# Attention heads in pairs on alternating row halves, and the bias added by VectorE while it takes the minimum

## What is computed

```
# layer 1 (odd): forgetting attention
log_f  = log_sigmoid(x @ w_f + forget_b)               # (S, 8)
cum    = cumsum(log_f, axis=1).transpose(0, 2, 1)
logits = q.k / sqrt(64) + cum[:, :, q0:q1, None] - cum[:, :, None, :q1]
probs  = softmax(where(causal, logits, -1e30));  y = probs @ v
# beside it: GLU -> causal depthwise conv (31 taps, 512 channels) -> LayerNorm -> swish

# layers 2, 3 (hybrid): a softmax over three dilated key patterns,
# equal to one softmax with a fixed bias log(count of patterns) per distance;
# beside it gated linear attention (4 heads), chunkwise
```

## Time and profile before

| | |
|---|---|
| Time, median of 3 runs | 1244.8 us (1244.3 to 1246.14) |
| Span of the profiled execution, first to last instruction | 1240.9 us |
| The profiled execution's own time around it | not given; its span is 3.9 us under the median of the runs |
| TensorE busy | 1216.8 us, 98% |
| VectorE, ScalarE, GpSimd busy | 763.0, 601.5, 37.8 us |
| Attention of layer 1 | about 340.5 to 380 us |
| Attention of layers 2 and 3 | about 682.3 to 705.1 and 1001 to 1024 us |

### The profile page before, as it was taken

How to read it: one execution, slowest core, us unless ns; L and a number is a source line. 1 busy time by engine, 2 the same in 40 slices (tenths; PEclk the granted TensorE clock), 3 DMA queues, 4 the chain that set the end, 5 groups by cost and what they waited for, 6 DMA issues and landing times.

```text
span 1240.9 us, 16942 instructions
## 1 busy us (share of the span) xinstructions
PE 1216.8 (98%) x5874; PEld 995.6 (80%) x5874; DVE 763.0 (61%) x1009; ACT 601.5 (48%) x911; POOL 37.8 (3%) x69
## 2 busy tenths in 40 slices
PE   7999999999999999999999999999999999999997
PEld 5778888888878788888778788888887878888886
DVE  5587545545976855554677766555465776755541
ACT  5455444525663544442465555444356563644430
POOL 0000000000000000000100110000010001000000
PEclk9999999999989999999999999999999999999999
DMA  8567666634701585573465239556626532765540
GB/s 283 169 204 228 219 196 196 222 108 157 247 22 60 180 282 172 179 242 122 136 204 161 70 105 292 173 179 216 213 74 202 181 105 86 232 208 172 178 159 34
DMA packets 162637, 212.99 MB, mean 172 GB/s; under 512 B 15817, under 2 KB 106601, under 8 KB 162576
## 3 DMA queue, kind: packets, MB, share of 16 engines
q1 hardware_dynamic: 155792, 201.44, 51.1%
q10 hardware_dynamic: 6784, 10.75, 2.8%
HBM read 211.09 MB, written 1.05 MB: 171 GB/s over the span
## 4 chain that ended last, share of the span: by engine, by line
PE 87%; DVE 5%; DMA 2%; ACT 2%; POOL 2%; issue 1%; ACTq 1%; SPq 0%; POOLq 0%; DVEq 0%
PE ps L538 25%; PE ps L540 25%; PE ps L539 25%; DMA raw<-ev_w_in 2%; PE ps L938 2%; PE ps L814 2%; DVE w_lo L1363 1%; PE ps L895 1%; PE ps L641 1%; PE ps L872 1%; PE ps L649 1%; PE ps L871 1%; POOL stat L1833 1%; PE ps L879 1%; ACT w_hi L990 1%
## 5 line engine op out<-in xcount | busy, mean ns | idle before, releaser
L1363 DVE TENSOR_TENSOR w_lo<-raw,w_hi 128x1024 fp32r<-128x1024 f32 x380 | 450.3, 1222 | 129.9 <-ACT w_hi L990 127.1
L990 ACT ACTIVATE w_hi<-raw 128x1024 fp32r<-128x1024 f32 x380 | 385.5, 1055 | 137.2 <-PE ps L540 72.7
L538 PE MATMUL ps<-w_hi,a_hi 128*128 128x512 f32 x1040 | 414.2, 398 | 4.2 <-ACT e_pc L1062 2.1
L540 PE MATMUL ps<-w_hi,a_lo 128*128 128x512 f32 x1040 | 406.8, 391 | 0.0
L539 PE MATMUL ps<-w_lo,a_hi 128*128 128x512 f32 x1040 | 405.7, 390 | 0.0
L538 PEld LDWEIGHTS ps<-w_hi,a_hi 128*128 128x128 f32 x1040 | 195.9, 188 | 46.1 <-issue 2.5
L540 PEld LDWEIGHTS ps<-w_hi,a_lo 128*128 128x128 f32 x1040 | 195.6, 188 | 42.2
L539 PEld LDWEIGHTS ps<-w_lo,a_hi 128*128 128x128 f32 x1040 | 196.1, 189 | 38.5
L538 PE MATMUL ps<-w_hi,h_hi 128*128 128x512 f32 x480 | 189.2, 394 | 0.9 <-DVE h_lo L1758 0.8
L540 PE MATMUL ps<-w_hi,h_lo 128*128 128x512 f32 x480 | 187.4, 390 | 0.0
L539 PE MATMUL ps<-w_lo,h_hi 128*128 128x512 f32 x480 | 187.3, 390 | 0.0
(11 more groups left out here) (205 smaller groups left out, 803.5 us busy)
## 6 DMA issues: line engine op xcount, KB each, us to landing
raw<-ffn_w_in SPq DMA_DIRECT2D x176, 256.0 KB, 4.3
raw<-w_in SPq DMA_DIRECT2D x96, 256.0 KB, 3.1
raw<-ffn_w_out SPq DMA_DIRECT2D x88, 256.0 KB, 4.1
raw<-w_gate SPq DMA_DIRECT2D x88, 256.0 KB, 3.6
raw<-w_up SPq DMA_DIRECT2D x88, 256.0 KB, 4.4
raw<-w_down SPq DMA_DIRECT2D x88, 256.0 KB, 4.1
raw<-od_w_in SPq DMA_DIRECT2D x40, 256.0 KB, 2.9
raw<-ev_w_in SPq DMA_DIRECT2D x32, 256.0 KB, 4.9
```

The source lines that it names most:

```text
L538: nc.tensor.matmul(ps[:, bank, :], hi, wh, start=first, stop=False)
L540: return nc.tensor.matmul(ps[:, bank, :], lo, wh, start=False, stop=last)
L990: nc.scalar.activation(w_hi[:, v.slot, :], raw[:, v.raw, :], ACT.Copy).then_inc(w_high, 1)
L1363: V.tensor_tensor(w_lo[:, v.slot, :], raw[:, v.raw, :], w_hi[:, v.slot, :].bitcast(F32), ALU.subtract).then_inc(w_low, 1)
```

## The change

- **Pairs.** `pair_logits(j)` computes near for heads 2j and 2j+1 and then wide for both, on the two row halves in turn. It waits for VectorE's `lows` of the pair before. TensorE's list becomes: `pair_logits(0)`, (linear_values), then for each j: `pair_logits(j+1)`, `head_turn(2j)`, `head_turn(2j+1)`, in layer 1 eight taps, `head_values(2j-2)`, `head_values(2j-1)`.
- **Bias.** The bias matmuls and their constants go. VectorE's `head_lows` reads the scores from PSUM, adds the bias, writes the sum to `probs` (now four buffers, in SBUF) and takes the minimum, in one instruction a part. ScalarE's exponentials work in place on `probs`.
- **Forget sums.** `cum` (8 x 256) is written to DRAM and read back broadcast to all partitions as `o_bias` (128 x 8 x 384, 1.5 MB), on ScalarE's DMA queue. GpSimd adds the causal mask in two instructions. `o_bias` lies over `rows[1]`, `rows[2]` and `nbuf`, so one load of a norm's row moves from layer 1's input projection to behind its attention.
- **Evictions.** In the hybrid layers ScalarE now copies even heads into `probsT`, VectorE odd ones. In layer 1 ScalarE copies all.
- **Feeds and convolution.** In the hybrid layers no unit is fed during attention; four are, after it. In layer 1 ScalarE feeds one unit for each pair, at its end. VectorE's convolution steps before attention go from 33 to 48.

```diff
@@ TensorE
+            def pair_logits(l, j):
+                if j:
+                    pe.wait_ge(lows.sem, lows.at(l, 2 * j - 1))
+                for i in range(2):
+                    r = slice(HD * i, HD * (i + 1))
+                    nc.tensor.matmul(tb[:, i, 0:P], qT[r, j, 0:P], kT[r, j, 0:P], start=True, stop=True)
+                for i in range(2):
+                    r = slice(HD * i, HD * (i + 1))
+                    nc.tensor.matmul(tb[:, i, P:3 * P], qT[r, j, P:SEQ], kT[r, j, :], start=True,
+                                     stop=True).then_inc(logits.sem, 1)
...
-                for h in range(HEADS):
-                    head_turn(l, h)
-                    if h + 2 < HEADS:
-                        head_logits(l, h + 2)
+                for j in range(HEADS // 2):
+                    if j + 1 < HEADS // 2:
+                        pair_logits(l, j + 1)
+                    head_turn(l, 2 * j)
+                    head_turn(l, 2 * j + 1)
                     if LAYERS[l] == "odd":
-                        fourth_block(range(4 * h, min(4 * h + 4, TAPS)))
-                    if h:
-                        head_values(l, h - 1)
-                    if LAYERS[l] == "hyb" and h == 4:
+                        fourth_block(range(8 * j, min(8 * j + 8, TAPS)))
+                    if j:
+                        head_values(l, 2 * j - 2)
+                        head_values(l, 2 * j - 1)
+                    if LAYERS[l] == "hyb" and j == 2:
                         turn_y(l, g_normed, 0)
+                head_values(l, HEADS - 2)
                 head_values(l, HEADS - 1)
@@ ScalarE
                     act.wait_ge(o_fcum.sem, o_fcum.at(1, 0))
-                    chain.step(nc.scalar.activation(o_cum[:, 0, 0:P], o_f[:, 1, 0:P], ACT.Copy))
-                    nc.scalar.activation(o_cum[:, 0, P:3 * P], o_f[:, 1, :], ACT.Copy).then_inc(o_cumhigh.sem, 1)
+                    act.dma_start(cum_rows, o_f[:, 1, :]).then_inc(cum_kept, 16)
...
                 feed(end)
                 if c == 2:
+                    act.wait_ge(cum_kept, 16)
+                    act.dma_start(o_bias[:, :, 0:P], cum_rows[:, 0:P].partition_broadcast(P)).then_inc(cum_spread, 16)
+                    act.dma_start(o_bias[:, :, P:3 * P], cum_rows.partition_broadcast(P)).then_inc(cum_spread, 16)
                     diagonals(range(N_DIAG))
...
             def attention(l):
+                for j in range(HEADS // 2):
+                    weights(l, 2 * j)
+                    weights(l, 2 * j + 1)
+                    turned_weights(l, 2 * j)
+                    if LAYERS[l] == "odd":
+                        turned_weights(l, 2 * j + 1)
+                        diagonals(range(8 * j + 8, min(8 * j + 16, TAPS)))
+                        feed(fed[0] + 1)
+                    if LAYERS[l] == "hyb" and j == 0:
                         linear_squares(l)
+                    if LAYERS[l] == "hyb" and j == 2:
                         split_y(l, (0, 1))
@@ VectorE
                 if c == 3:
+                    convolve(8)
                     feed(end)
-                    convolve(5)
+                    convolve(6)
                 if c == 4:
+                    convolve(6)
                     feed(end)
...
             def head_lows(l, h):
+                at = h % N_PROBS
                 dve.wait_ge(logits.sem, logits.at(l, h))
+                if h >= N_PROBS:
+                    dve.wait_ge(p_turned.sem, p_turned.at(l, h - N_PROBS))
+                for t, part in enumerate((slice(0, P), slice(P, 3 * P))):
+                    bias = o_bias[:, h, part] if LAYERS[l] == "odd" else const[:, C_DIL + part.start:C_DIL + part.stop]
+                    ins = V.tensor_tensor_reduce(probs[:, at, part], tb[:, h % 2, part], bias, 1.0, -3.0 * MASKED, ALU.add, ALU.min,
+                                                 low_of[:, at, t:t + 1])
...
+                head_lows(l, 0)
+                head_lows(l, 1)
+                for j in range(HEADS // 2):
+                    beside(2 * j)
+                    if j + 1 < HEADS // 2:
+                        head_lows(l, 2 * j + 2)
+                        head_lows(l, 2 * j + 3)
+                    if LAYERS[l] == "hyb":
+                        h = 2 * j + 1
+                        dve.wait_ge(p_turned.sem, p_turned.at(l, h))
+                        if h >= 2:
+                            dve.wait_ge(attended.sem, attended.at(l, h - 2))
+                        V.tensor_copy(probsT[:, h % 2, :], tb[:, 2 + h % 2, 0:3 * P]).then_inc(p_odd_v.sem, 1)
+                    beside(2 * j + 1)
@@ GpSimd
+                    pool.wait_ge(const_in, 16 * 2)
+                    pool.wait_ge(cum_spread, 16 * 2)
+                    causal = const[:, C_CAUSAL:C_CAUSAL + P].unsqueeze(1).broadcast_to([P, HEADS, P])
+                    chain.step(nc.gpsimd.tensor_tensor(o_bias[:, :, 0:P], o_bias[:, :, 0:P], causal, ALU.add))
+                    nc.gpsimd.tensor_tensor(o_bias[:, :, 2 * P:3 * P], o_bias[:, :, 2 * P:3 * P], causal, ALU.add).then_inc(o_masked.sem, 1)
```

More of the change, by code:

```diff
@@ L178, in blocks_kernel @@
         h_lo, at_hl = place("h_lo", [P, KF, SEQ], F32R)
-        rows, _ = place("rows", [P, 3, D], F32)
+        rows, at_rows = place("rows", [P, 3, D], F32)
         nbuf, _ = place("nbuf", [P, D], F32)
@@ L220, in blocks_kernel @@
         y_tok = scratch("y_tok", [P, NT, CH], 6)
-        probs = late("probs", [P, 2, 3 * P], 0)
-        probsT = late("probsT", [P, 2, 3 * P], 3072)
+        N_PROBS = 4
+        probs = late("probs", [P, N_PROBS, 3 * P], 0)
+        probsT = late("probsT", [P, 2, 3 * P], 6144)
+        o_bias, _ = place("o_bias", [P, HEADS, 3 * P], F32, at_rows + 4 * D)
+        cum_rows = nc.dram_tensor("cum_rows", (GATES, SEQ), F32, kind="Internal").ap()
         e_pc = scratch("e_pc", [P, NT, CH], 0)
@@ L454, in blocks_kernel, with p_out @@
         LEVELS_AFTER = {1: (0, 1), 2: (2, 3, 4), 3: (5, 6), 4: (7,)}
+        def p_out(l, h):
+            return p_even if h % 2 == 0 else p_odd_a if LAYERS[l] == "odd" else p_odd_v
         def right(ap, m):
@@ L1009, in load_rows @@
                 for slot, col, row in norm_rows(k):
-                    act.dma_start(rows[:, slot, col:col + row.shape[0]], row.partition_broadcast(P)).then_inc(rows_in, 16)
+                    if (k, slot) != (2, 1):
+                        act.dma_start(rows[:, slot, col:col + row.shape[0]], row.partition_broadcast(P)).then_inc(rows_in, 16)
             def boundary(k, t):
@@ L1132, in odd_rest @@
                 attention(1)
-                turned_weights(1, HEADS - 1)
+                for slot, col, row in norm_rows(2)[1:]:
+                    act.dma_start(rows[:, slot, col:col + row.shape[0]], row.partition_broadcast(P)).then_inc(rows_in, 16)
                 act.wait_ge(o_tapped.sem, o_tapped.at(1, TAPS - 1))
@@ L1228, in turned_weights @@
                     act.wait_ge(attended.sem, attended.at(l, h - 2))
-                nc.scalar.activation(probsT[:, h % 2, :], tb[:, 2 + h % 2, 0:3 * P], ACT.Copy).then_inc(p_out.sem, 1)
-            def attention(l):
[L1232 to L1241, removed]
+                nc.scalar.activation(probsT[:, h % 2, :], tb[:, 2 + h % 2, 0:3 * P], ACT.Copy).then_inc(p_out(l, h).sem, 1)
@@ new lines, in weights @@
+            def weights(l, h):
+                at = h % N_PROBS
+                act.wait_ge(lows.sem, lows.at(l, h))
+                for t, part in enumerate((slice(0, P), slice(P, 3 * P))):
+                    ins = nc.scalar.activation(probs[:, at, part], probs[:, at, part], ACT.Exp, scale=-1.0,
+                                               bias=low_of[:, at, t:t + 1], accum_out=total[:, t, h:h + 1])
+                ins.then_inc(weighed.sem, 1)
+            def attention(l):
+                for j in range(HEADS // 2):
[7 more added lines that the diff above has]
+                    if LAYERS[l] == "hyb" and j == 0:
@@ L1553, in odd_step @@
                 if c == 2:
-                    dve.wait_ge(o_cumhigh.sem, o_cumhigh.at(1, 0))
-                    for at, n in ((0, P), (P, SEQ)):
-                        ins = V.tensor_tensor(o_cum[:, 1, at:at + n], o_f[:, 1, 0:n], o_cum[:, 0, at:at + n].bitcast(F32), ALU.subtract)
-                        if at == 0:
-                            chain.step(ins)
-                    ins.then_inc(o_cumlow.sem, 1)
                     convolve(8)
@@ new lines, in head_lows @@
+                for t, part in enumerate((slice(0, P), slice(P, 3 * P))):
+                    bias = o_bias[:, h, part] if LAYERS[l] == "odd" else const[:, C_DIL + part.start:C_DIL + part.stop]
+                    ins = V.tensor_tensor_reduce(probs[:, at, part], tb[:, h % 2, part], bias, 1.0, -3.0 * MASKED, ALU.add, ALU.min,
+                                                 low_of[:, at, t:t + 1])
+                    if t == 0:
+                        chain.step(ins)
+                ins.then_inc(lows.sem, 1)
```

57 lines of the change are left out of this document (14 added, 43 removed).

## The result

The kernel after takes 1270.2 us (median of 4 runs, 1267.7 to 1271.3) beside 1244.6 for the kernel before (4 runs, 1243.2 to 1246.1): ratio 1.0197, 95% interval 1.0182 to 1.0211. The forecast was 1261.1, range 1246 to 1274, slower at 0.82. The profiled execution took 1270.35 with a span of 1267.7, 26.8 more than before.

The account below looks back on a forecast made before the run. TensorE, holding 87% of the chain of waits, was taken as the bound. Layer 1's 7.6, its clock's 5.1 and the hybrid layers' 3.6 made +16.3 on the 1240.9 span; with 3.9 around it, 1261.1 us, range 1246 to 1274.

Parts of the forecast that it names:

- The ring: Layer 1's attention: ScalarE's copies wait for values behind eight taps, so the engines take turns; 10.8 us a pair against 9.26.
- The entry: Start of layer 1's attention: 15 more convolution steps (6.1 us), less 0.6, put VectorE's entry at 345.8 instead of 340.3.
- covered likewise: GpSimd's two mask adds, 2.5 us each, ready at 345 before VectorE's entry into layer 1's attention, so costing nothing.
- The fused add-and-minimum: VectorE's new instruction in attention, not in the trace: taken at 0.53 us a head, like the reductions it replaces.
- The clock in layer 1: TensorE idles 3.4 us in each of three passes; three clock falls at 1.7 us each, plus 5.1.
- Layer 1's sum: Layer 1's whole loss: 7.6 us from late entry, alternating engines and end, plus 5.1 for the clock.
- the tail: End of layer 1's attention, after the last pass at 384.2: copies 1.1, conversion 1.1, issue and semaphores 1.2, to 387.6.
- Layers 2 and 3: Hybrid attention: late GpSimd root, minima behind linear_norm and exponentials behind y's split cost 1.8 us a layer, 3.6 together.
- the upper bound: Worst case for each hybrid layer: plus 3.5 us, with one clock fall of the smaller kind.
- rival 3: Layer 1's engines take turns and every clock fall costs 3.4: 1266, or 1270 with one in each hybrid layer; chance 0.15.
- I take the pair as serial: Query-key products of two heads on the two row halves run one after the other, 1.74 us a pair with mode changes.
- rival 5: Products on the two row halves run together, while layer 1's engines still take turns: 1257; chance 0.07.

Follow-up runs that it names:

- e1: Kernel after, with layer 1's values of heads 2j-2 and 2j-1 issued ahead of the eight taps instead of behind them: 1262.2 us, ratio to before 1.014.
- e2: Kernel after, with GpSimd's two causal mask adds left out and a tiny copy signalling in their place: 1267.0 us.
- e5: Kernel after, with useless TensorE products where it waited in layers 2 and 3, lists unchanged: 1257.1 us, ratio to before 1.0097.
- e4: Kernel after, hybrid layers reordered: linear squares ahead of ScalarE's first copy, y's split behind the last exponentials, next minima ahead of linear_norm: 1250.5 us.
- e10: Kernel after with lists reordered in all three layers (1232.4 us), then 15 convolution steps moved back from ahead of layer 1's attention into it: 1234.2 us.
- e7: Kernel after, with pair_logits issuing both products of the first head, then both of the second: 1270.2 us in one run.

## Why the prediction came out as it did

- **The ring** was right in place, cause and members, and the waits on ScalarE and TensorE's idling (3.9 and 4.5 us against 3.4) are there; e1 shows it by breaking it. A turn took 12.8, not 10.8, the difference being the half-speed clock in turns and taps (5.0 for eight taps, against 3.3).
- **The entry** failed by its first term: 350.25, less the 1.5 by which everything is late, is 348.7 against 345.8. I had costed the adds at nothing as long as they ended in time (they ended at 346.1, 344.6 less the shift, against my 345). But they run beside work of VectorE with two inputs in SBUF, and 3.3 us of delay pass through them (e2): the step that failed is "covered likewise".
- **The fused add-and-minimum** at 0.53 a head: 0.55 (two heads from 350.25 to 351.36).
- **The clock in layer 1**, three falls at 1.7: two more than before, of 6 us and more each, and a longer first. (1 - 0.78) x 53.3 = 11.7 us are lost at it where the earlier trace rows give (1 - 0.92) x 42.8 = 3.4: 8.3 more against 5.1. A part of it lies beside ScalarE's chain.
- **Layer 1's sum**, 12.7 forecast and 13.5 measured, is in part luck. Counted along the chain and without the 1.5 of the start, the first values ended 2.3 later than forecast, for which the sum had nothing; the two turns took 4.6 more, where it had 5.1 for the clock; the tail was 0.7 shorter. So 1.2 of the missing 2.3 is offset by terms that were too high.
- **Layers 2 and 3**, 1.8 each: here is the miss, 6.4 and 5.4. The waits I worked out came where I put them (GpSimd's root, minima behind linear_norm, exponentials behind the split of y), if not with their sizes (0.65 ahead of pair_logits(3) against 1.5), but the sum left the clock out. A fall there stood only in the upper bound (+3.5 in all, so 1.7 for the fall) and in rival 3. It cost at least 5.9 to 6.9 (e5).
- **"I take the pair as serial"** was wrong, and rival 5 right on it: 0.86, not 1.74 with the mode change. The Trainium skill (TensorE: Matmul & The Clock Gate, Part 3: Packing small matmuls — row/col tiling) says that matmuls on different row groups run at the same time. It was right against my reading; this case's trace agrees with it, and a pair took 0.88 less than my sum, not the 0.43 less that I worked out by the rule. TensorE's removed work was thus 10.6 us larger over twelve pairs. The kernel was slower all the same, as the lists made TensorE wait; how much of the 10.6 reached the time, no run shows.

Added up, 13.5 + 6.4 + 5.4 + 1.5 (start) = 26.8 against the sum of 16.3. Rival 3 (1266 to 1270, 0.15) came nearest, by its number more than its terms: its 1270 has 1.7 in each hybrid layer, and with its own 3.4 a fall it would be 1273. The entry's 2.9 is in none of its terms.

## What to carry to other kernels

When work is taken from the engine that bounds a kernel, walk each other engine's list and ask which instruction now stands behind which wait; here the same instructions gave 2% slower or 1% faster by their order alone. TensorE's waits of up to 1.8 us between short products had two prices in this kernel, their own length (at most 3.7 us a hybrid layer, e5 against e4) and the clock behind them (5.9 to 6.9): count the second wherever a sparse stretch gets sparser. Useless products in the holes tell the two apart in one run.

## What was not expected of the hardware

- GpSimd's first add of 128x1024 took 6.62 us beside VectorE's subtractions `w_lo` of 128x1024, which kept their pace (four in 4.63 us). Beside the convolution steps it was the other way round: the second add took 2.18, and two steps took 2.2 each in place of 0.41, so that the twelve lost 3.5 us. In e10, beside the same subtractions, the two adds took 2.00 and 3.00, and three subtractions 7.0 in place of 3.5. No profile shows an add of this size with VectorE idle. The Trainium skill (SBUF — State Buffer, Who interferes with whom) says that a VectorE instruction with two inputs in SBUF contends with a GpSimd instruction that reads SBUF, and calls the ports they share an exclusive lock. This trace agrees: one or the other loses, and what the first add lost, 6.62 less some 2, is the length of the four subtractions.
- Two 64-row products on different halves start some 10 ns apart and end together, in either order of issue (0.86 us for two heads, 0.85 for one), and a product can start ahead of one on the other half that was issued before it (e7).
- 20 us at 1.2 GHz with TensorE busy for 17.8 of them (708.5 to 728.5): once the clock has fallen, short products at half speed fill the time and look busy, so the busy share does not show the loss; the granted clock does.
